# Who turns two of the ten blocks of a head's probabilities in the second layer

## The chip, the cores and the metric

One core of a Trainium2 chip runs the whole program. The metric is the time on the device in microseconds, the median of several runs; lower is better. A core has five engines with instruction queues of their own, which meet only at semaphores: TensorE (PE, the matrix unit; PEld are its weight loads), VectorE (DVE), ScalarE (ACT), GpSimd (POOL) and SyncE (SP, which here only starts DMAs). SBUF is the on-chip memory of 128 partitions, PSUM the memory of eight banks into which PE writes; DVE and ACT can read both.

## What is computed

A residual stack of two layers on 512 tokens of width 1024, with 8 heads of 128. Layer 0 is block-sparse attention, which with two blocks of 256 keys comes to causal attention, with rotary q and k. Layer 1, the second layer, is the forgetting attention. Cut to what matters:

```python
# layer 1, x is (1, 512, 1024)
hdn = rms_norm(x, norm_g[1])
proj = hdn @ b_w_in                          # q, k, v, z of 8 heads, and a forget logit for each head
q, k = rms_norm(q, b_q_norm), rms_norm(k, b_k_norm)
c = cumsum(log_sigmoid(f_logit + b_f_bias))  # along the tokens
s = q @ k.T * 128 ** -0.5 + (c[:, None] - c[None, :])   # causal: keys up to the query
y = softmax(s) @ v
x = x + (y * silu(z)) @ w_out[1]             # all in float32
```

## The kernel before

**Numbers.** The products are float32 in accuracy but are made of three products each of a high and a low part: for an operand X, ACT writes `X_hi`, the value rounded to PE's format, and DVE or POOL writes `X_lo`, the rest. `three` (L379 to L381) issues hi*hi, hi*lo, lo*hi.

**Tiles.** The 512 tokens are four tiles of 128. A head's scores are causal: query tile t has keys 0 to 128 (t + 1), so a head has ten blocks of 128x128. The probabilities lie in SBUF as `probs`, query tiles one after the other, queries on the partitions. For the product with v, keys must lie on the partitions, so each block is turned: `turn_probs` (L488) lets PE multiply it with an identity (L495), ten times, into the PSUM banks of `PT_AT`, grouped by key tile: group 0 is key tile 0 (512 columns), group 1 key tile 1 (384), group 2 key tiles 2 and 3 (256 + 128 columns next to each other in bank 5). Each group raises `p_turned`. ACT's `split_probs` copies a group from PSUM to `pT_hi` (L715, `pThi_set`), DVE's `split_probs` subtracts that from the group for `pT_lo` (L988, `pTlo_set`), and PE's `values` waits for all three groups and makes y in bank 3 (L509).

**The loop.** Each engine runs its own `period(layer, h, s)`: head 0 apart, then a hardware loop over heads 1 to 6 with two of them in a body, then `last` for head 7. In one period an engine works on the attention of head h, on the projection of head h + 1 and on the weights of head h + 2:
- PE: qkv of head h + 1 for token tiles 0 and 1, `scores` of head h, qkv for tiles 2 and 3, `turn_probs`, `zproj` (the gate z of head h + 1), `values`. qkv of a tile waits until `norm_qk` two tiles before it has freed its bank (`qkn_set`), and tile 0 of a head for its weights (`wlo_set`).
- DVE: `gate_y` of head h - 1, `split_qk` (L954, qkT_lo), `split_v` and `norm_qk` (L902, L919) of tile 0, `maxima` (L972), the same for tile 1, `invert_sums`, `low_y`, `silu_part` (L1013, L1017), `split_v` and `norm_qk` of tile 2, `split_v` of tile 3, `split_probs`, `norm_qk` of tile 3, and `turn_qk` (L947): q and k of head h + 1 turned from `qkn` into PSUM in sixteen STREAM_TRANSPOSE instructions. Each of them moves one block row and column of 32 partitions by 32 columns, for eight such squares at once.
- ACT: `split_qk` (L699, qkT_hi), `split_y` (L727, yT_hi), `read_qkv` of tile 0 (L684, sums of squares, and L693, v_hi) and of tile 1, `exps` (L706) and `normalise` (L722) which make the probabilities in the order of query tiles 3, 2, 1, 0 (`probs_set` each), `read_qkv` of tiles 2 and 3, `split_probs`, with the eight chunks of `split_w` (L638, w_hi of head h + 2) spread between; chunks 6 and 7 stand behind `split_probs`.
- POOL: the rstd of each tile (L1185, L1187, from ACT's sums to DVE's `norm_qk`), the eight chunks w_lo (L1160), and `mask_bias` (L1252), which adds the row of c to the causal mask for the maxima of the next head.

`r_row` is an SBUF buffer of 128x512, filled once and read in layer 0 alone (`scale_z`, L910).

Of the kernel before, what the change touches and what calls it, by code (L numbers as in the profile page):

```python
# [12 lines left out]
P = 128  # L13
SEQ = 512
DM = 1024
HEADS = 8
LAYERS = 2
TILES = SEQ // P
# [17 lines left out]
ALU = mybir.AluOpType  # L36
ACT = mybir.ActivationFunctionType
# [5 lines left out]
PT_AT = {0: (3, 0), 1: (4, 0), 2: (5, 0), 3: (5, 256)}  # L43
P_COL = {t: sum(P * (u + 1) for u in range(t)) for t in range(TILES)}
# [2 lines left out]
POOL_FIRST = {1: 2, 2: 1, 4: 2, 6: 2, 7: 1}  # L47
DVE_FIRST = (0, 3, 5)
NEXT_W = ((3, 4), (5, 6), (7,), ())
QUAD = 32  # L50
QUADS = P // QUAD


def build_trunk(nc, x, norm_g, w_out, a_w_in, a_q_norm, a_k_norm, b_w_in, b_f_bias, b_q_norm,
                b_k_norm, rope_cos, rope_sin, out):
    with ExitStack() as ctx:
# [3 lines left out]
        def sem(name):  # L60
            return ctx.enter_context(nc.semaphore(name))
# [22 lines left out]
        probs = sb("probs", [P, TRI])  # L84
        pT_hi = sb("pT_hi", [P, TRI], F32R)
# [79 lines left out]
        rinv_set = sem("rinv_set")  # L165
        probs_set = sem("probs_set")
        p_turned = sem("p_turned")
        pThi_set = sem("pThi_set")
        pTlo_set = sem("pTlo_set")
        y_done = sem("y_done")  # L170
# [24 lines left out]
        def f32(ap):  # L195

            return ap.bitcast(F32)
# [58 lines left out]
        def scaled_count(layer, t):  # L256

            return (TILES - UNSCALED + t if layer else t - UNSCALED) + 1

        def heads_loop(eng, layer, first, period, last):  # L260

# [112 lines left out]
        def _(pe):  # L374
# [113 lines left out]
            def turn_probs(layer, h):  # L488
                g = HEADS * layer + h
                pe.wait_ge(probs_set, TILES * (g + 1))  # L490
                for js in PT_GROUPS:
                    for j in js:
                        bank, col = PT_AT[j]
                        for t in range(j, TILES):
                            mm = pe.transpose(banks[:, bank, col + (t - j) * P:col + (t - j + 1) * P],  # L495
                                              probs[:, P_COL[t] + j * P:P_COL[t] + (j + 1) * P], ident[:, :])
                    mm.then_inc(p_turned, 1)
# [123 lines left out]
        def _(act):  # L621
# [87 lines left out]
            def split_probs(layer, h):  # L709
                g = HEADS * layer + h  # L710
                for n, js in enumerate(PT_GROUPS):
                    w = sum(SEQ - j * P for j in js)
                    c = PT_COL[js[0]]
                    act.wait_ge(p_turned, 3 * g + n + 1)
                    act.activation(pT_hi[:, c:c + w], banks[:, PT_AT[js[0]][0], 0:w], ACT.Copy).then_inc(pThi_set, 1)  # L715

            def normalise(layer, h):
                g = HEADS * layer + h
# [115 lines left out]
        def _(dve):  # L834
# [59 lines left out]
            def split_v(layer, h, s, t):  # L894
                a = TILES * (HEADS * layer + h) + t
                dve.wait_ge(vhi_set, a + 1)
                v = banks[:, qkv_bank(layer, h, t), 2 * P:3 * P]
                if unscaled(layer, t):
                    dve.scalar_tensor_tensor(out=v_lo[:, s, t, :], in0=v, scalar=r_raw[:, t:t + 1], in1=f32(v_hi[:, s, t, :]),
                                             op0=ALU.mult, op1=ALU.subtract).then_inc(vlo_set, 1)  # L900
                else:
                    dve.tensor_tensor(v_lo[:, s, t, :], v, f32(v_hi[:, s, t, :]), ALU.subtract).then_inc(vlo_set, 1)  # L902
# [9 lines left out]
            def norm_qk(layer, h, t):  # L912

                a = TILES * (HEADS * layer + h) + t
                dve.wait_ge(rstd_set, a + 1)
                wait(dve, qkn_set, a - 1)
                if layer == 1:
                    for m in range(2):
                        last = dve.scalar_tensor_tensor(out=qkn[:, t, m, :], in0=banks[:, qkv_bank(layer, h, t), m * P:(m + 1) * P],  # L919
                                                        scalar=rstd[:, t % 2, m:m + 1], in1=cos_t[:, 0, m, :],  # L920
                                                        op0=ALU.mult, op1=ALU.mult)
                    last.then_inc(qkn_set, 1)
                    return
                for m in range(2):
                    swapped = banks[:, qkv_bank(layer, h, t), m * P:(m + 1) * P].rearrange("p (a n) -> p a n", a=2)[:, ::-1, :]
                    dve.scalar_tensor_tensor(out=rot[:, t % 2, m].rearrange("p (a n) -> p a n", a=2), in0=swapped,
                                             scalar=rstd[:, t % 2, m:m + 1],
                                             in1=sin_t[:, t, m].rearrange("p (a n) -> p a n", a=2),
                                             op0=ALU.mult, op1=ALU.mult).then_inc(rot_set, 1)
                dve.wait_ge(rot_set, 4 * a + 2)  # L930
                for m in range(2):
                    part = banks[:, qkv_bank(layer, h, t), m * P:(m + 1) * P]
                    dve.scalar_tensor_tensor(out=part, in0=part, scalar=rstd[:, t % 2, m:m + 1], in1=cos_t[:, t, m],
                                             op0=ALU.mult, op1=ALU.mult).then_inc(rot_set, 1)
                dve.wait_ge(rot_set, 4 * a + 4)
                dve.tensor_tensor(qkn[:, t, :, :], banks[:, qkv_bank(layer, h, t), 0:2 * P].rearrange("p (m n) -> p m n", m=2),
                                  rot[:, t % 2, :, :], ALU.add).then_inc(qkn_set, 1)
# [44 lines left out]
            def split_probs(layer, h):  # L982
                g = HEADS * layer + h
                for n, js in enumerate(PT_GROUPS):
                    w = sum(SEQ - j * P for j in js)
                    c = PT_COL[js[0]]
                    dve.wait_ge(pThi_set, 3 * g + n + 1)
                    dve.tensor_tensor(pT_lo[:, c:c + w], banks[:, PT_AT[js[0]][0], 0:w], f32(pT_hi[:, c:c + w]),  # L988
                                      ALU.subtract).then_inc(pTlo_set, 1)

            def gate_y(layer, h):

# [108 lines left out]
            def period(layer, h, s):  # L1101
                begin(layer, h)
                split_v(layer, h + 1, 1 - s, 0)
                norm_qk(layer, h + 1, 0)
                maxima(layer, h)
                if layer == 0:
                    scale_z(layer, h)
                split_v(layer, h + 1, 1 - s, 1)
                norm_qk(layer, h + 1, 1)
                invert_sums(layer, h)  # L1110
                if layer == 1:
                    late_y(layer, h)
                for n in range(4):
                    silu_part(layer, h, n)
                split_v(layer, h + 1, 1 - s, 2)
                norm_qk(layer, h + 1, 2)
                split_v(layer, h + 1, 1 - s, 3)
                split_probs(layer, h)
                norm_qk(layer, h + 1, 3)
                turn_qk(layer, h + 1)  # L1120
# [198 lines left out]
```

## Time and profile before

| what | us |
|---|---|
| median of 3 runs | 547.85 |
| lowest and highest run | 547.60, 548.28 |
| the profiled execution, its own time | 548.04 |
| span of the profiled execution | 546.0 |
| PE busy / DVE busy in the span | 538.5 / 411.2 |
| ACT busy / POOL busy in the span | 293.3 / 301.6 |
| granted clock of PE, mean | 0.999 |

The time of a run lies about 2 us above the span, which begins with the first instruction of the program and ends with the last. Busy times are sums over the whole program; what counts is which engine waits for which at the place of the change, and for that the rows below go through one head in order of time. The second layer's loop takes from about 313 us to 502 us of the span. A row of the timeline is one instruction, or several of the same line in a row with their common length.

### The profile page before, as it was taken

What the parts mean: (1) busy time and instruction counts of PE and PEld (TensorE: products, weight loads), DVE (VectorE), ACT (ScalarE), POOL (GpSimd) and SP (SyncE); (2) the same over time, 40 slices, a digit from 0 to 9 for tenths busy, and PEclk for the clock granted to TensorE, in tenths of its full rate; (3) what the DMA queues carried; (4) which work ended last, traced back from release to release, by engine and by line L of the source; (5) the groups of instructions that cost most, each with busy time, mean ns of one, the idle gap of its engine ahead of it and who ended that gap; (6) DMA issues with size and microseconds to landing.
All of it is one profiled execution on the core that took longest, in us unless ns stands there. A gap on an engine that the chain in (4) does not pass through costs nothing.

```text
span 546.0 us, 9781 instructions
## 1 busy us (share of the span) xinstructions
PE 538.5 (99%) x2963; PEld 498.4 (91%) x2963; DVE 411.2 (75%) x1042; ACT 293.3 (54%) x863; POOL 301.6 (55%) x357
## 2 busy tenths in 40 slices
PE   6999999999999999999999999999999999999998
PEld 5999999999999999888898999999999999998887
DVE  4678999999999999973563777878787878788331
ACT  6748282928282828272545473737374747464400
POOL 3874564646464646453645486747474747476300
PEclk9999999999999999999999999999999999999999
DMA  9914323231313131223513345525241534232021
GB/s 262 250 27 127 101 59 97 59 97 58 96 58 96 58 96 59 95 86 118 128 27 80 97 102 74 120 61 130 52 121 54 116 57 121 73 105 84 26 96 59
DMA packets 78540, 50.22 MB, mean 92 GB/s; under 512 B 4256, under 2 KB 71592, under 8 KB 78512
## 3 DMA queue, kind: packets, MB, share of 16 engines
q1 hardware_dynamic: 78496, 49.87, 33.8%
q8 instruction: 14, 0.23, 0.2%
q14 instruction: 14, 0.11, 0.1%
q10 hardware_dynamic: 16, 0.00, 0.0%
HBM read 47.75 MB, written 2.12 MB: 91 GB/s over the span
## 4 chain that ended last, share of the span: by engine, by line
PE 97%; DMA 1%; ACT 0%; DVE 0%; SPq 0%; issue 0%
PE banks L379 27%; PE banks L381 27%; PE banks L380 27%; PE banks L509 6%; PE banks L495 3%; PE banks L484 2%; PE banks L483 2%; PE banks L482 2%; DMA first_raw<-in_a_w_in_dram 1%; PE banks L416 1%; PE banks L536 0%; PE banks L535 0%; ACT hT_hi L670 0%; PE banks L467 0%; SPq L333 0%; DVE w_lo L885 0%
## 5 line engine op out<-in xcount | busy, mean ns | idle before, releaser
L1160 POOL TENSOR_TENSOR w_lo<-w_raw,w_hi 128x512 fp32r<-128x512 f32 x146 | 188.4, 1305 | 84.0 <-ACT w_hi L638 84.0
L379 PE MATMUL banks<-w_hi,hT_hi 128*128 128x384 f32 x512 | 173.5, 339 | 0.5 <-DVE w_lo L885 0.3
L381 PE MATMUL banks<-w_hi,hT_lo 128*128 128x384 f32 x512 | 171.8, 336 | 0.0
L380 PE MATMUL banks<-w_lo,hT_hi 128*128 128x384 f32 x512 | 171.8, 335 | 0.0
L947 DVE STREAM_TRANSPOSE banks<-qkn 32x256 f32<-32x256 f32 x240 | 109.4, 456 | 3.6
L379 PEld LDWEIGHTS banks<-w_hi,hT_hi 128*128 128x128 f32 x512 | 96.7, 189 | 2.3 <-DVE w_lo L885 0.7
L380 PEld LDWEIGHTS banks<-w_lo,hT_hi 128*128 128x128 f32 x512 | 96.7, 189 | 0.6
L381 PEld LDWEIGHTS banks<-w_hi,hT_lo 128*128 128x128 f32 x512 | 96.5, 189 | 0.0
L684 ACT ACTIVATE junk<-banks 128x128 bf16<-128x128 f32 x128 | 34.0, 272 | 112.0 <-PE banks L381 111.8
L638 ACT ACTIVATE w_hi<-w_raw 128x512 fp32r<-128x512 f32 x148 | 89.0, 638 | 8.9 <-PE banks L381 5.4
L1013 DVE RECIPROCAL gz<-gz 128x128 f32<-128x128 f32 x64 | 54.3, 908 | 0.7 <-ACT gz L736 0.7
L379 PE MATMUL banks<-w_hi,yT_hi 128*128 128x512 f32 (+1 forms) x136 | 51.8, 381 | 0.0
L381 PE MATMUL banks<-w_hi,yT_lo 128*128 128x512 f32 (+1 forms) x136 | 51.3, 377 | 0.0
L380 PE MATMUL banks<-w_lo,yT_hi 128*128 128x512 f32 (+1 forms) x136 | 51.2, 377 | 0.0
L379 PE MATMUL banks<-hT_hi,w_hi 128*128 128x512 f32 x128 | 51.1, 399 | 0.0
L381 PE MATMUL banks<-hT_hi,w_lo 128*128 128x512 f32 x128 | 50.0, 390 | 0.0
L380 PE MATMUL banks<-hT_lo,w_hi 128*128 128x512 f32 x128 | 49.9, 390 | 0.0
L1187 POOL TENSOR_TENSOR rstd<-msq,power 128x2 f32<-128x2 f32 x64 | 45.2, 705 | 5.0
L706 ACT ACTIVATE probs<-probs,negmax 128x512 f32<-128x512 f32 (+1 forms) x64 | 35.2, 553 | 6.6 <-DVE negmax L972 5.7
L699 ACT ACTIVATE qkT_hi<-banks 128x512 fp32r<-128x512 f32 x32 | 17.5, 603 | 37.3 <-DVE banks L947 37.3
L1185 POOL TENSOR_TENSOR msq<-ssq,eps 128x2 f32<-128x2 f32 x32 | 6.4, 200 | 55.0 <-ACT junk L684 55.0
L1185 POOL TENSOR_TENSOR msq<-ssq,eps_raw 128x2 f32<-128x2 f32 x32 | 7.2, 224 | 53.5 <-ACT junk L684 53.5
(119 smaller groups left out, 915.9 us busy)
## 6 DMA issues: line engine op xcount, KB each, us to landing
w_raw<-in_b_w_in_dram SPq DMA_DIRECT2D x64, 256.0 KB, 3.6
w_raw<-in_a_w_in_dram SPq DMA_DIRECT2D x52, 256.0 KB, 2.9
w_raw<-in_w_out_dram SPq DMA_DIRECT2D x32, 256.0 KB, 2.7
first_raw<-in_a_w_in_dram SPq DMA_DIRECT2D x12, 256.0 KB, 5.7
cos_t<-c_rows SPq DMA_DIRECT2D x8, 256.0 KB, 3.6
out_dram<-xs SPq DMA_DIRECT2D x7, 256.0 KB, 2.0
xs<-in_x_dram SPq DMA_DIRECT2D x3, 512.0 KB, 5.9
xs<-in_x_dram SPq DMA_DIRECT2D x2, 256.0 KB, 3.1
```

The lines of the kernel that those rows point to most:

```text
L379: pe.matmul(dst, ah, bh, start=first and m == 0, stop=False)
L380: pe.matmul(dst, ah, bl, start=False, stop=False)
L381: mm = pe.matmul(dst, al, bh, start=False, stop=last and m == n - 1)
L509: mm = pe.matmul(banks[:, Y_BANK, j * P:SEQ], a[:, s, j, :], b[:, PT_COL[j]:PT_COL[j] + w], start=n == 0, stop=n == len(work) - 1)
L638: act.activation(w_hi[:, slot, k, :], raw, ACT.Copy).then_inc(whi_set, 1)
L684: sq = act.activation(junk[:, m, :], banks[:, qkv_bank(layer, h, t), m * P:(m + 1) * P], ACT.Square, scale=SCALE, accum_out=ssq[:, t % 2, ...
L699: act.activation(qkT_hi[:, m, :], banks[:, QT_BANK + m, :], ACT.Copy).then_inc(qkThi_set, 1)
L706: act.activation(part, part, ACT.Exp, bias=negmax[:, t:t + 1], scale=-1.0, accum_out=rowsum[:, t:t + 1]).then_inc(exp_set, 1)
L947: at = dve.transpose(turned[:, :, :, a * QUAD:(a + 1) * QUAD], tokens[:, :, :, b * QUAD:(b + 1) * QUAD])
L1013: dve.reciprocal(part, part).then_inc(ez1_set, 1)
L1160: pool.tensor_tensor(w_lo[:, slot, k, :], raw, f32(w_hi[:, slot, k, :]), ALU.subtract).then_inc(wlo_set, by)
L1187: pool.tensor_tensor(rstd[:, t % 2, :], msq[:, t % 2, :], power[:, :], ALU.pow).then_inc(rstd_set, 1)
```

## The change

In heads 0 to 6 of layer 1, the two blocks of query tile 3 with key tiles 2 and 3 are no longer turned by PE. DVE turns them: `turn_last_probs` is a new function with sixteen transposes of 32 partitions by two squares of 32 columns, from `probs` into columns 128 to 384 of `r_row`, which raises `last_turned`. It stands behind `norm_qk` of tile 2 and ahead of `split_v` of tile 3, and waits until query tile 3 of the probabilities is normalised. PE's `turn_probs` leaves out the two blocks. Group 2 is now 128 columns in PSUM and 256 columns in `r_row`, so ACT and DVE split it in two instructions; ACT's second one waits for `last_turned`. Group 2's signals `pThi_set` and `pTlo_set` are raised by the second one. Layer 0 and head 7 are as before. FIRST_BY_DVE = 2 is the first key tile that DVE turns.

```diff
--- before.py
+++ after.py
@@ -47,6 +47,7 @@
 POOL_FIRST = {1: 2, 2: 1, 4: 2, 6: 2, 7: 1}
 DVE_FIRST = (0, 3, 5)
 NEXT_W = ((3, 4), (5, 6), (7,), ())
+FIRST_BY_DVE = 2
 QUAD = 32
 QUADS = P // QUAD
 
@@ -165,6 +166,7 @@
         rinv_set = sem("rinv_set")
         probs_set = sem("probs_set")
         p_turned = sem("p_turned")
+        last_turned = sem("last_turned")
         pThi_set = sem("pThi_set")
         pTlo_set = sem("pTlo_set")
         y_done = sem("y_done")
@@ -257,6 +259,14 @@
 
             return (TILES - UNSCALED + t if layer else t - UNSCALED) + 1
 
+        def late_part(js):
+
+            return r_row[:, 0:P] if js[0] == 1 else r_row[:, P:3 * P]
+
+        def by_dve(layer, h):
+
+            return layer == 1 and not (isinstance(h, int) and h == HEADS - 1)
+
         def heads_loop(eng, layer, first, period, last):
 
 
@@ -492,6 +502,8 @@
                     for j in js:
                         bank, col = PT_AT[j]
                         for t in range(j, TILES):
+                            if by_dve(layer, h) and t == TILES - 1 and j >= FIRST_BY_DVE:
+                                continue
                             mm = pe.transpose(banks[:, bank, col + (t - j) * P:col + (t - j + 1) * P],
                                               probs[:, P_COL[t] + j * P:P_COL[t] + (j + 1) * P], ident[:, :])
                     mm.then_inc(p_turned, 1)
@@ -712,7 +724,12 @@
                     w = sum(SEQ - j * P for j in js)
                     c = PT_COL[js[0]]
                     act.wait_ge(p_turned, 3 * g + n + 1)
-                    act.activation(pT_hi[:, c:c + w], banks[:, PT_AT[js[0]][0], 0:w], ACT.Copy).then_inc(pThi_set, 1)
+                    late = P * sum(j >= FIRST_BY_DVE for j in js) if by_dve(layer, h) else 0
+                    hi = act.activation(pT_hi[:, c:c + w - late], banks[:, PT_AT[js[0]][0], 0:w - late], ACT.Copy)
+                    if late:
+                        act.wait_ge(last_turned, h + 1)
+                        hi = act.activation(pT_hi[:, c + w - late:c + w], late_part(js), ACT.Copy)
+                    hi.then_inc(pThi_set, 1)
 
             def normalise(layer, h):
                 g = HEADS * layer + h
@@ -985,8 +1002,30 @@
                     w = sum(SEQ - j * P for j in js)
                     c = PT_COL[js[0]]
                     dve.wait_ge(pThi_set, 3 * g + n + 1)
-                    dve.tensor_tensor(pT_lo[:, c:c + w], banks[:, PT_AT[js[0]][0], 0:w], f32(pT_hi[:, c:c + w]),
-                                      ALU.subtract).then_inc(pTlo_set, 1)
+                    late = P * sum(j >= FIRST_BY_DVE for j in js) if by_dve(layer, h) else 0
+                    lo = dve.tensor_tensor(pT_lo[:, c:c + w - late], banks[:, PT_AT[js[0]][0], 0:w - late],
+                                           f32(pT_hi[:, c:c + w - late]), ALU.subtract)
+                    if late:
+                        part = slice(c + w - late, c + w)
+                        lo = dve.tensor_tensor(pT_lo[:, part], late_part(js), f32(pT_hi[:, part]), ALU.subtract)
+                    lo.then_inc(pTlo_set, 1)
+
+            def turn_last_probs(layer, h):
+
+                g = HEADS * layer + h
+                dve.wait_ge(probs_set, TILES * g + 1)
+                row = P_COL[TILES - 1]
+                for js in ((1,), (2, 3)):
+                    if js[0] < FIRST_BY_DVE:
+                        continue
+                    n = len(js)
+                    tokens = probs[:, row + js[0] * P:row + (js[-1] + 1) * P].rearrange("p (j c) -> p j c", j=n)
+                    keys = late_part(js).rearrange("p (j c) -> p j c", j=n)
+                    for a in range(QUADS):
+                        for b in range(QUADS):
+                            turned = dve.transpose(keys[b * QUAD:(b + 1) * QUAD, :, a * QUAD:(a + 1) * QUAD],
+                                                   tokens[a * QUAD:(a + 1) * QUAD, :, b * QUAD:(b + 1) * QUAD])
+                turned.then_inc(last_turned, 1)
 
             def gate_y(layer, h):
 
@@ -1114,6 +1153,8 @@
                     silu_part(layer, h, n)
                 split_v(layer, h + 1, 1 - s, 2)
                 norm_qk(layer, h + 1, 2)
+                if by_dve(layer, h):
+                    turn_last_probs(layer, h)
                 split_v(layer, h + 1, 1 - s, 3)
                 split_probs(layer, h)
                 norm_qk(layer, h + 1, 3)
```

On DVE, head 0 of layer 1, from the reciprocals of the gate to the turning of q and k, before:

```order
L1013 RECIPROCAL gz<-gz 128x128 x4
L1017 TENSOR_TENSOR gz<-banks,gz 128x512
L902 TENSOR_TENSOR v_lo<-banks,v_hi 128x128
L919 SCALAR_TENSOR_TENSOR qkn<-banks,rstd,cos_t 128x128 x2
L902 TENSOR_TENSOR v_lo<-banks,v_hi 128x128
L988 TENSOR_TENSOR pT_lo<-banks,pT_hi 128x512
L988 TENSOR_TENSOR pT_lo<-banks,pT_hi 128x384 x2
L919 SCALAR_TENSOR_TENSOR qkn<-banks,rstd,cos_t 128x128 x2
L947 STREAM_TRANSPOSE banks<-qkn 32x8x32 x16
```

The same stretch now (line numbers of the changed kernel):

```order
L1052 RECIPROCAL gz<-gz 128x128 x4
L1056 TENSOR_TENSOR gz<-banks,gz 128x512
L919 TENSOR_TENSOR v_lo<-banks,v_hi 128x128
L936 SCALAR_TENSOR_TENSOR qkn<-banks,rstd,cos_t 128x128 x2
L1026 STREAM_TRANSPOSE r_row<-probs 32x2x32 x16
L919 TENSOR_TENSOR v_lo<-banks,v_hi 128x128
L1006 TENSOR_TENSOR pT_lo<-banks,pT_hi 128x512
L1006 TENSOR_TENSOR pT_lo<-banks,pT_hi 128x384
L1006 TENSOR_TENSOR pT_lo<-banks,pT_hi 128x128
L1010 TENSOR_TENSOR pT_lo<-r_row,pT_hi 128x256
L936 SCALAR_TENSOR_TENSOR qkn<-banks,rstd,cos_t 128x128 x2
L964 STREAM_TRANSPOSE banks<-qkn 32x8x32 x16
```

Sixteen transposes from `probs` stand ahead of v_lo of tile 3 and of all pT_lo, and the third pT_lo is two instructions. The loop over heads 1 to 6 has the same order.

On ACT, head 0 of layer 1, the probabilities' high parts and what follows, before:

```order
L693 ACTIVATE v_hi<-banks 128x128
L715 ACTIVATE pT_hi<-banks 128x512
L715 ACTIVATE pT_hi<-banks 128x384 x2
L638 ACTIVATE w_hi<-w_raw 128x512 x2
L734 ACTIVATE gz<-banks 128x512
```

And now:

```order
L705 ACTIVATE v_hi<-banks 128x128
L728 ACTIVATE pT_hi<-banks 128x512
L728 ACTIVATE pT_hi<-banks 128x384
L728 ACTIVATE pT_hi<-banks 128x128
L731 ACTIVATE pT_hi<-r_row 128x256
L650 ACTIVATE w_hi<-w_raw 128x512 x2
L751 ACTIVATE gz<-banks 128x512
```

The 256-wide copy from `r_row`, which waits for DVE, stands ahead of the last two chunks of the weights. On PE the ten turns in a row are eight, at the same place.

## Rows read from the trace of the kernel before

**Rows 1.** The page: busy time by engine; the chain that ended last.

```profile
PE 538.5 (99%) x2963; PEld 498.4 (91%) x2963; DVE 411.2 (75%) x1042; ACT 293.3 (54%) x863; POOL 301.6 (55%) x357
...
PE 97%; DMA 1%; ACT 0%; DVE 0%; SPq 0%; issue 0%
```

**Rows 2.** Stretch 310 to 500: length, busy PE, PEld, DVE, ACT, POOL; clock; DMA.

```profile
310.00:500.00 190.00, 190.00 (x1076) 180.35 (x1075) 148.81 (x389) 110.12 (x341) 123.44 (x145) 1.00 0.37 87
```

**Rows 3.** Timeline of PE: start, length, instruction, shapes, count.

```profile
377.66 1.25 PE L495 MATMUL banks<-ident,probs 128*128 128x128 f32 x10
378.67 0.48 PE L379 MATMUL banks<-hT_hi,w_hi 128*128 128x512 f32 x1
...
384.20 0.56 PE L509 MATMUL banks<-pT_hi,v_hi 128*128 128x512 f32 x2
...
386.12 0.34 PE L379 MATMUL banks<-w_hi,hT_hi 128*128 128x384 f32 x1
...
394.47 0.39 PE L482 MATMUL banks<-qkT_hi 128*128 128x512 f32 x1
...
492.42 0.56 PE L509 MATMUL banks<-pT_hi,v_hi 128*128 128x512 f32 x2
...
501.82 0.39 PE L482 MATMUL banks<-qkT_hi 128*128 128x512 f32 x1
```

**Rows 4.** Timeline of DVE in head 2; in brackets idle time before, and releaser.

```profile
376.54 0.61 DVE L919 SCALAR_TENSOR_TENSOR qkn<-banks,rstd,cos_t 128x128 f32<-128x128 f32 x2
378.68 0.29 DVE L902 TENSOR_TENSOR v_lo<-banks,v_hi 128x128 fp32r<-128x128 f32 x1 [1.54 <-ACT v_hi L693]
379.17 1.62 DVE L988 TENSOR_TENSOR pT_lo<-banks,pT_hi 128x512 fp32r<-128x512 f32 x3 [0.20 <-ACT pT_hi L715]
380.71 0.60 DVE L919 SCALAR_TENSOR_TENSOR qkn<-banks,rstd,cos_t 128x128 f32<-128x128 f32 x2
381.34 7.50 DVE L947 STREAM_TRANSPOSE banks<-qkn 32x256 f32<-32x256 f32 x16
...
389.51 1.29 DVE L954 TENSOR_TENSOR qkT_lo<-banks,qkT_hi 128x512 fp32r<-128x512 f32 x2
...
392.52 0.61 DVE L919 SCALAR_TENSOR_TENSOR qkn<-banks,rstd,cos_t 128x128 f32<-128x128 f32 x2 [0.76 <-POOL rstd L1187]
395.38 0.69 DVE L972 CUSTOM_DVE_ANT_0 probs<-banks,sin_t 128x512 f32<-128x512 f32 x1 [2.24 <-issue]
```

**Rows 5.** Groups by shape, 310 to 500: count, busy us, mean ns, idle before.

```profile
L947 DVE STREAM_TRANSPOSE banks<-qkn 32x256 f32<-32x256 f32 x113 | 51.5, 456 | 1.7
L988 DVE TENSOR_TENSOR pT_lo<-banks,pT_hi 128x384 fp32r<-128x384 f32 x14 | 7.1, 547 | 0.0
L988 DVE TENSOR_TENSOR pT_lo<-banks,pT_hi 128x512 fp32r<-128x512 f32 x7 | 4.8, 692 | 1.4 <-ACT pT_hi L715 1.4
...
L972 DVE CUSTOM_DVE_ANT_0 probs<-banks,sin_t 128x512 f32<-128x512 f32 x7 | 4.8, 687 | 12.2 <-issue 12.2
...
L972 DVE CUSTOM_DVE_ANT_0 probs<-banks,sin_t 128x128 f32<-128x128 f32 x7 | 2.0, 285 | 0.0
...
L722 ACT ACTIVATE probs<-probs,rinv 128x256 f32<-128x256 f32 x7 | 3.5, 495 | 0.0
```

**Rows 6.** Timeline of ACT in head 2.

```profile
371.77 1.91 ACT L722 ACTIVATE probs<-probs,rinv 128x512 f32<-128x512 f32 x4
...
389.85 0.63 ACT L727 ACTIVATE yT_hi<-gz 128x512 f32 x1
390.64 0.28 ACT L684 ACTIVATE junk<-banks 128x128 bf16<-128x128 f32 x1 [0.16 <-PE banks L381]
```

**Rows 7.** Timeline of POOL in head 2: w_lo 6 and 7.

```profile
380.50 2.55 POOL L1160 TENSOR_TENSOR w_lo<-w_raw,w_hi 128x512 fp32r<-128x512 f32 x2 [0.58 <-ACT w_hi L638]
```

**Rows 8.** Timeline of PE and DVE in head 0.

```profile
313.31 0.39 PE L482 MATMUL banks<-qkT_hi 128*128 128x512 f32 x1
...
316.38 0.06 DVE L971 MEMSET gate<- 1x1 f32 x1 [2.92 <-POOL sin_t L1252]
...
324.64 0.61 DVE L919 SCALAR_TENSOR_TENSOR qkn<-banks,rstd,cos_t 128x128 f32<-128x128 f32 x2 [0.78 <-POOL rstd L1187]
...
330.10 0.56 PE L509 MATMUL banks<-pT_hi,v_hi 128*128 128x512 f32 x2
```

## The prediction

> **What bounds the kernel now.** I read the page first. TensorE (PE) is busy for 99% of the span and makes 97% of the chain that ended last [rows 1]. In the second layer it never waits: between 310 and 500 us it is busy for all 190.00 us [rows 2]. So work taken from PE shortens the run one for one, as long as nothing makes PE wait instead. VectorE (DVE) is busy for 75% of the span and for 148.81 us of those 190, so it is idle for 22% of them [rows 1, 2]. The reader should look next at where that idle time lies, because only idle time at the right place can pay for new work.
>
> I call the heads of the second layer head 0 to head 7. One round of the loop takes PE 27.05 us: the values of head 2 start at 384.20, those of head 6 at 492.42, and (492.42 - 384.20) / 4 = 27.05 [rows 3]. The rows of DVE in head 2 show three large pieces of idle time in such a round: 1.54 us before v_lo of query tile 3, 0.76 us before norm_qk 0, 2.24 us before the maxima [rows 4]. The second one is a wait for POOL, which itself starts behind ACT and DVE: it moves along with a delay and absorbs nothing.
>
> **PE's part.** Ten turns of probabilities take from 377.66 to 378.67, 0.10 us each [rows 3]; the first product behind them also ends later than usual (0.48 us), so I count 0.105. Two of ten go in heads 0 to 6: 0.21 us a head, **1.5 us** in all. Nothing hides this gain, since PE is the bound. PE's round becomes 26.84 us. Head 7 stays as it is.
>
> **DVE's part.** Sixteen transposes of 32x64 a head are new. The trace has only the 32x256 kind: 456 ns each, and sixteen of them last 7.50 us, so (7.50 - 0.46) / 15 = 0.470 us from start to start: they don't overlap at all [rows 4, 5]. Other instructions of DVE do: three pT_lo of 692, 547 and 547 ns take 1.54 us up to the next start, 0.08 us less for each than their length [rows 4, 5]. What does a narrow transpose cost? The maxima take 285 ns for 128 columns and 687 for 512, which is 1.05 ns a column and 151 ns fixed [rows 5]. Taking 192 columns off a wide transpose gives 0.470 - 0.201 = 0.27 us. If its fixed part were those 151 ns too, a column would cost 1.19 ns and a narrow one 0.24 us. If narrow ones overlapped as pT_lo does, it would be 0.151 + 0.067 - 0.08 = 0.14 us, the lower end. At the upper end a narrow one costs as much as a wide one, 0.47 us; with nothing that makes columns free here I leave that end only a trace of a chance. I take 0.26 us, between 0.24 and 0.27 and nearer to the straight subtraction, thus **4.2 us a head**.
>
> That transposes don't overlap is also what the Trainium skill says in "VectorE: DVE Perf Modes", section "Two Vector instructions with no wait between them": an instruction whose output starts in another group of 32 partitions than the one before is held until everything before it has finished. By that rule, the trace's 470 ns agree, and the new loop, which also changes that group at each step, would be held too. The same page's section on the TRN2 errata has 58 cycles plus the columns for work from SBUF to SBUF; as an estimate from it a narrow one would be 127 ns and the whole 2.0 us a head, and the run would gain the full 1.5 us. The 456 ns of the wide ones speak against it.
>
> The third pT_lo and the third pT_hi (128x384) become a 128-wide and a 256-wide instruction each. From start to start that is 0.20 + 0.34 us on DVE where one 384-wide takes 0.47: 0.07 us more. On ACT the 256-wide copy from SBUF has 495 ns by the row of the same shape [rows 5], in place of two thirds of the old 384-wide one: some 0.2 us more. The wait for probabilities ahead of the transposes costs nothing: they are ready at 371.77 + 1.91 = 373.68 [rows 6], DVE comes at 377.07.
>
> **A steady head, walked through (times of head 2).** The transposes start behind norm_qk 2, at 377.07, and end at 381.25. v_lo, pT_lo 0, pT_lo 1 and the two parts follow in steps of 0.20, 0.61, 0.47 and 0.20 us, so the last part starts at 382.73 and pT_lo is complete at 383.15. norm_qk 3 starts 0.34 us after that part, at 383.07 instead of 380.71: 2.37 us late. PE wants pT_lo at 384.20 - 0.21 = 383.99 [rows 3, 4]. Covered, with 0.8 us to spare. Behind it turn_qk (7.50 us) moves from 381.34 to 383.71, and qkT_lo ends at 393.17 instead of 390.80; PE's scores want it at 394.47 - 0.21 = 394.26. Covered. ACT's yT_hi goes to 392.22 and its read of tile 0 to 392.75, 2.11 late (before it had waited some 0.26 us for PE) [rows 6]; so norm_qk 0 goes from 392.52 to 394.63, and DVE is ready for the maxima at 395.15. PE's scores allow them at 395.38 - 0.21 = 395.17. **DVE's round, through ACT and POOL, is then 26.83 us, PE's 26.84.** All the absorbing idle time is used up, and a head that starts late can't catch up any more.
>
> The third pT_hi waits for DVE until 381.25. Queued behind it on ACT stand w_hi 6 and 7, and behind those on POOL w_lo 6 and 7 (380.50 to 383.05) [rows 7]. They move by 1.9 us to about 385.0; PE needs them for the next tile at 386.12 - 0.21 = 385.91 [rows 3]. Covered with 0.9 us in a head on time, but with only 0.1 us in one where PE has already waited for pT_lo.
>
> **Head 0 is not steady.** There PE's scores start at 313.31 but DVE's maxima at 316.4, because they wait 2.92 us for the bias that POOL makes: 3.1 us behind, where it is 0.9 us later on. norm_qk 2 starts at 324.64, PE's values at 330.10 [rows 8]. With the change the transposes run from 325.17 to 329.37, pT_lo is complete 1.90 us later, at 331.27, and PE starts its values at 331.32 instead of 330.10 - 0.21 = 329.89. **PE waits 1.4 us**, once. From then on PE sits right behind pT_lo, and since DVE's round equals PE's it stays there, without further waits in heads 1 to 6 if 0.26 is right.
>
> **Head 7** has less work for PE between values and scores: from 492.42 to 501.82 are 9.40 us, in the loop from 384.20 to 394.47 10.27 [rows 3]. From a complete pT_lo to a complete qkT_lo DVE takes 393.17 - 383.15 = 10.02 us. Behind a head 6 at the edge these scores wait up to 0.6 us. I take 0.5, since six heads have won back some hundredths each.
>
> **Sum:** -1.5 + 1.4 + 0.5 = +0.4 us on the profiled run of 548.04 (span 546.0), which lies 0.19 us over the median of the runs, 547.85. On the median that is **548.3 us**. A measurement of this kernel can tell some 0.2%, 1.1 us; this is less.
>
> How it hangs on the narrow transpose: each 0.01 us of it is 0.16 us in head 0, and above 0.26 it is another 0.16 us in each of the six heads behind.
> - 0.14 us: no waits, -1.5.
> - 0.24 us: 1.1 us in head 0; DVE wins back 0.3 us a head, so no wait in head 7: -0.4.
> - 0.27 us: 1.6 + 6 x 0.15 + 0.6 - 1.5 = +1.6.
> - 0.28 us: 1.75 + 6 x 0.31 + 0.6 - 1.5 = +2.7.
>
> **Rivals.**
> 1. The loop through DVE becomes the bound (slower). Its place is the wait for pTlo_set ahead of the values, in each of heads 1 to 6. It decides from about 0.265 us a transpose, or from any 0.1 us a round that my walk lacks. For it: the straight subtraction gives 0.27 and my margin is 0.01 us. Against it: the fixed part of every other kind is 151 ns, which gives 0.24. It gives 549.0 to 550.6, in the middle 549.6. Chance 0.32.
> 2. Narrow transposes are cheap and overlap, 0.14 to 0.20 us. PE waits 0.4 us at most, in head 0: 546.4 to 546.8. For it: other instructions of DVE overlap. Against it: no wide transpose does. Chance 0.10. The Trainium skill, "Vector Engine (DVE) Microarchitecture Reference", section 5.2, has about 1.04 ns a column and 75 ns for each instruction, an estimate of 142 ns with the same outcome; no row here shows it for transposes.
> 3. POOL's w_lo 7 is late rather than pT_lo. Its place is PE's first tile behind the values. It needs 0.1 us more on ACT or POOL than I have and gives 0.1 to 0.3 us a head: 548.6 to 550. Chance 0.05, half of it beyond 1.1 us.
> 4. That the change does not do what it says is excluded by the order of the instructions: eight turns on PE and sixteen transposes on DVE stand where ten turns stood.
>
> **How the numbers follow.** Forecast (547.2 to 548.9) 0.53, rival 1 0.32, rival 2 0.10, rival 3 0.05. Faster by over 0.2% (below 546.75) is nearly all of rival 2: 0.09. Slower by over 0.2% (above 548.95) is rival 1 nearly whole and half of rival 3: 0.33. Within 0.2%: 0.58. The range takes the forecast, rival 1 up to a transpose of 0.28 us less a little, and the slower half of rival 2: 546.7 to 550.4.
>
> **What would show it.** Right: transposes from probs 245 to 255 ns long and 0.26 us apart behind norm_qk 2; PE's first wait ahead of the values of head 0, 1.4 us, released by DVE's pT_lo; none or tiny ones in heads 1 to 6; one ahead of the scores of head 7; DVE's idle time before the maxima near 0 where it was 2.24 us; DVE's busy share up from 75% to about 80%. Wrong: no wait in head 0 (rival 2), waits ahead of the values of every head (rival 1), or waits ahead of the first tile with POOL as releaser (rival 3).

## The result, and the profile after

The changed kernel takes 551.86 us (median of 6 runs, 551.56 to 552.67) beside 547.92 for the kernel before (6 runs, 547.60 to 549.10). The ratio is 1.007, with a 95% interval of 1.0057 to 1.0083: it is 3.9 us slower. I had forecast 548.3 and at most 550.4.

The page of the changed kernel shows PE at 98% and DVE at 80%. The chain that ended last was PE for 97% before [rows 1]; now DVE and POOL hold a share of it:

```profile
PE 538.7 (98%) x2949; PEld 495.4 (90%) x2949; DVE 440.8 (80%) x1161; ACT 293.2 (53%) x870; POOL 302.3 (55%) x357
...
PE 58%; DVE 20%; POOL 9%; issue 8%; ACT 3%; DMA 1%; POOLq 0%; SPq 0%; ACTq 0%; DVEq 0%
```

The waits of PE's weight loads say where. Each row gives what was waited for, then the us in total, how often, and the longest. Seven waits for the last part of pT_lo stand ahead of the values, one for qkT_lo ahead of the scores:

```profile
PEld banks L521 <- DVE pT_lo L1010: 5.9, 7, 2.1
...
PEld banks L492 <- DVE qkT_lo L971: 0.8, 1, 0.8
```

PE's timeline shows when the values of a head start: here for heads 0, 1, 2 and 6, and in the last row the scores of head 7. The idle time in brackets is how PE arrives there, after a weight load that had stood waiting.

```profile
331.80 0.68 PE L521 MATMUL banks<-pT_hi,v_hi 128*128 128x512 f32 x2 [1.72 <-DVE pT_lo L1010]
...
359.12 0.68 PE L521 MATMUL banks<-pT_hi,v_hi 128*128 128x512 f32 x2 [0.15 <-DVE pT_lo L1010]
...
386.43 0.68 PE L521 MATMUL banks<-pT_hi,v_hi 128*128 128x512 f32 x2 [0.17 <-DVE pT_lo L1010]
...
495.74 0.50 PE L521 MATMUL banks<-pT_hi,v_hi 128*128 128x512 f32 x1 [0.22 <-DVE pT_lo L1010]
...
505.75 0.50 PE L492 MATMUL banks<-qkT_hi 128*128 128x512 f32 x1 [0.34 <-DVE qkT_lo L971]
```

Head 0 starts its values at 331.80, where the prediction's walk had 329.89 without a wait: 1.9 us. From 331.80 to 495.74 are six rounds of 27.32 us, where PE alone would need the 26.84 of the prediction: 0.48 us in each, 2.9 together. Head 7's scores come 10.01 us after head 6's values, before it was 9.40 [rows 3]: 0.6. With 1.4 us taken from PE (measured below) that is 1.9 + 2.9 + 0.6 - 1.4 = +4.0, and the runs say 3.9.

What is slow in the round of DVE? Its groups by shape between 310 and 505 us (count, busy us, mean ns, idle before):

```profile
L1026 DVE STREAM_TRANSPOSE r_row<-probs 32x64 f32<-32x64 f32 x112 | 26.4, 236 | 1.4
...
L1010 DVE TENSOR_TENSOR pT_lo<-r_row,pT_hi 128x256 fp32r<-128x256 f32 x7 | 7.9, 1122 | 0.0
```

The transposes are a little cheaper than forecast, 236 ns long where the prediction had 245 to 255. The subtraction of 256 columns, which I had put at 0.34 us from start to start, takes 1122 ns. The timeline of head 2 shows what runs beside it: DVE in the first fence, POOL in the second, ACT in the third.

```profile
379.78 3.97 DVE L1026 STREAM_TRANSPOSE r_row<-probs 32x64 f32<-32x64 f32 x16
383.78 0.29 DVE L919 TENSOR_TENSOR v_lo<-banks,v_hi 128x128 fp32r<-128x128 f32 x1
383.99 1.34 DVE L1006 TENSOR_TENSOR pT_lo<-banks,pT_hi 128x512 fp32r<-128x512 f32 x3
385.24 1.13 DVE L1010 TENSOR_TENSOR pT_lo<-r_row,pT_hi 128x256 fp32r<-128x256 f32 x1
386.30 0.60 DVE L936 SCALAR_TENSOR_TENSOR qkn<-banks,rstd,cos_t 128x128 f32<-128x128 f32 x2
```

```profile
380.62 1.30 POOL L1201 TENSOR_TENSOR w_lo<-w_raw,w_hi 128x512 fp32r<-128x512 f32 x1 [0.16 <-ACT w_hi L650]
...
384.80 2.72 POOL L1201 TENSOR_TENSOR w_lo<-w_raw,w_hi 128x512 fp32r<-128x512 f32 x2 [1.95 <-ACT w_hi L650]
...
386.04 1.48 POOL L1201 TENSOR_TENSOR w_lo<-w_raw,w_hi 128x512 fp32r<-128x512 f32 x1
```

```profile
383.78 0.42 ACT L731 ACTIVATE pT_hi<-r_row 128x256 fp32r<-128x256 f32 x1 [1.52 <-DVE r_row L1026]
384.10 0.61 ACT L650 ACTIVATE w_hi<-w_raw 128x512 fp32r<-128x512 f32 x1
```

The second POOL row is w_lo 6 and w_lo 7 together, the third is w_lo 7 alone. w_lo 6 runs from 384.80 to 386.09. DVE's subtraction starts inside it, at 385.24, and ends at 386.37, 0.28 us behind it. w_lo 7, which starts before DVE is done, takes 1.48 us, and the two chunks together last 2.72 us where they lasted 2.55 [rows 7]. In all seven heads the subtraction starts about 0.45 us behind w_lo 6 and takes 1.10 to 1.13 us. The change itself brings the two together: ACT now waits for DVE's transposes before its last pT_hi, and w_hi 6 and 7 are queued behind that, so POOL gets w_hi 6 just before DVE reaches the subtraction.

### The profile page after: what moved, and what is told of

Same layout as the page of the kernel before. It is cut to its first block, busy times and chain, and to the rows that moved or that the text cites. A ratio compares the mean times of both kernels' runs of the same rounds, so it can differ in the third digit from the quotient of the medians.

```text
span 550.1 us, 9885 instructions
## 1 busy us (share of the span) xinstructions
PE 538.7 (98%) x2949; PEld 495.4 (90%) x2949; DVE 440.8 (80%) x1161; ACT 293.2 (53%) x870; POOL 302.3 (55%) x357
## 4 chain that ended last, share of the span: by engine, by line
PE 58%; DVE 20%; POOL 9%; issue 8%; ACT 3%; DMA 1%; POOLq 0%; SPq 0%; ACTq 0%; DVEq 0%
PE banks L389 16%; PE banks L391 16%; PE banks L390 16%; DVE banks L964 10%; POOL w_lo L1201 6%; DVE r_row L1026 4%; PE banks L521 3%; PE banks L507 2%; POOL rstd L1228 2%; DVE qkn L936 2%; DVE pT_lo L1010 1%; DVE pT_lo L1006 1%; DMA first_raw<-in_a_w_in_dram 1%; PE banks L494 1%; PE banks L493 1%
```

## The experiments

**Theory A**: the 256-wide subtraction, with both inputs in SBUF, stands still while POOL's w_lo runs. **Rival B**: `r_row` is slow to read, by its place in SBUF or because it was just written. **Rival C**: pT_hi, which ACT has just written, is slow to read, so the loss has nothing to do with where the first input lies.

Besides the runs' time I give the **stretch** from the start of head 0's scores to that of head 7's, read from PE's timeline. It leaves out the start of the program, which varies between executions: head 0's scores start between 312.76 us (experiment 6) and 314.52 us (experiment 3) in the profiled ones. The mean granted clock of PE is 1.00 in every profiled execution. The stretch of the kernel before is 501.82 - 313.31 = 188.51 us [rows 3, 8], that of the changed kernel 505.75 - 313.33 = 192.42.

Each ratio is to the kernel before on the same chip. Its medians there were 547.89 us for experiments 1 to 4, 548.21 for 5 to 8, 548.04 for 9 and 10, and 548.74 for 11. Experiments 2, 3 and 4 were run once, so their times carry no interval.

**1. PSUM in the place of r_row.** One line:

```diff
-            return r_row[:, 0:P] if js[0] == 1 else r_row[:, P:3 * P]
+            return banks[:, QT_BANK, 2 * P:3 * P] if js[0] == 1 else banks[:, QT_BANK, 0:2 * P]
```

> The changed kernel with one line other: DVE turns the two blocks into PSUM bank 6 (free between the splitting of q and k and their next turning) and no longer into r_row in SBUF, so the 256-wide pT_lo has one input in PSUM and one in SBUF. In the changed kernel this instruction takes 1122 ns where its columns explain 420; in all seven heads it starts 0.45 us after a w_lo of POOL, which also reads two SBUF inputs, and ends 0.28 us after it. Theory A (a DVE instruction with two SBUF inputs waits for a running one of POOL): 420 ns here, DVE's round 27.32 - 0.70 = 26.62 us, below PE's 26.84; PE waits 1.2 us ahead of the values of head 0 and not in heads 1 to 6; in all -1.5 + 1.2 + 0 to 0.2, so 547.6 us. Rival B (r_row is slow to read, by its place or because it was just written): the same, 547.6. Rival C (pT_hi, just written by ACT, is what is slow to read): 1.1 us for the instruction as before, 551.9 us.

Measured: 550.37 us (549.68 to 551.31), ratio 1.004 (1.0027 to 1.0053), stretch 190.54. The groups of DVE:

```profile
L1010 DVE TENSOR_TENSOR pT_lo<-banks,pT_hi 128x256 fp32r<-128x256 f32 x7 | 2.9, 414 | 0.0
...
L1026 DVE STREAM_TRANSPOSE banks<-probs 32x64 f32<-32x64 f32 x112 | 28.7, 256 | 1.6
```

The subtraction falls from 1122 to 414 ns with POOL beside it as before (in head 2 it starts at 386.10, inside a w_lo that starts at 385.62 and takes 1.29 us). It still reads pT_hi, so C is out. A and B both fit. But the time is far from the 547.6 that I expected. The transposes into PSUM take 256 ns instead of 236, 0.33 us more for sixteen, and the first of them starts 0.64 us behind norm_qk 2 instead of 0.53. These 0.44 us bring DVE's round from the expected 26.62 to some 27.05 us, still 0.21 over PE's. 1.65 in head 0 + 6 x 0.21 + 0.6 in head 7 - 1.4 = +2.1, and the stretch has grown by 2.0. Half of the loss is gone, and what is left is a new cost that the experiment itself brought in.

**2. POOL's chunks 6 and 7 cut to 16 columns** in the second layer (the rest of these w_lo isn't computed):

```diff
+                    if layer == 1 and k >= 6 and not (isinstance(h, int) and h < 2):
+                        pool.tensor_tensor(w_lo[:, slot, k, 0:16], raw[:, 0:16], f32(w_hi[:, slot, k, 0:16]),
+                                           ALU.subtract).then_inc(wlo_set, by)
+                        continue
```

> The changed kernel with POOL's last two chunks of w_lo of layer 1 (from head 2's weights on) cut to 16 of 512 columns; the other columns keep old values, so this part of the computation is left out. DVE's instructions are those of the changed kernel. Theory A: with POOL idle at that time the 256-wide pT_lo from r_row takes 420 ns, PE has no waits ahead of the values of heads 1 to 6, 547.6 us. Rivals B and C: it stays at 1.1 us, 551.9 us.

Measured: 547.92 us in one run, stretch 188.42. DVE's row in head 2, and POOL's two short chunks:

```profile
383.77 0.42 DVE L1010 TENSOR_TENSOR pT_lo<-r_row,pT_hi 128x256 fp32r<-128x256 f32 x1
```

```profile
383.33 0.22 POOL L1202 TENSOR_TENSOR w_lo<-w_raw,w_hi 128x16 fp32r<-128x16 f32 x1 [1.78 <-ACT w_hi L650]
383.99 0.28 POOL L1202 TENSOR_TENSOR w_lo<-w_raw,w_hi 128x16 fp32r<-128x16 f32 x1 [0.43 <-ACT w_hi L650]
```

DVE's program is unchanged to the last instruction, `r_row` and `pT_hi` lie where they lay, and the subtraction takes 416 ns in the mean of seven (414 to 417). So B and C are out, and A is what is left. PE waits for pT_lo once, in head 0, for 1.0 us on PE's timeline. This run costs 4.0 us of stretch less than the changed kernel: that is the price of the standing still, in the seven heads together. It is less than 7 x 0.70 us because without it PE's own round is the longer one again. What is left without it is 188.42 against 188.51, -0.1 us, where the prediction's sum said +0.4.

**3. One input instead of two** (the subtraction is left out; pT_lo becomes a rounded copy):

```diff
-                        lo = dve.tensor_tensor(pT_lo[:, part], late_part(js), f32(pT_hi[:, part]), ALU.subtract)
+                        lo = dve.tensor_scalar(pT_lo[:, part], late_part(js), 1.0, None, ALU.mult)
```

> The changed kernel with the 256-wide pT_lo made from r_row alone (times 1.0, the subtraction of pT_hi is left out), so it reads one SBUF input. Theory A (two SBUF inputs are needed for the wait): 300 to 420 ns, 547.5 us. Rival B (r_row is slow): 1.1 us, 551.9. Rival C (pT_hi is slow): like A.

Measured: 552.43 us in one run, stretch 191.61. In head 2, DVE and then POOL:

```profile
386.25 1.00 DVE L1010 TENSOR_SCALAR pT_lo<-r_row 128x256 fp32r<-128x256 f32 x1
```

```profile
385.80 2.60 POOL L1201 TENSOR_TENSOR w_lo<-w_raw,w_hi 128x512 fp32r<-128x512 f32 x2 [1.89 <-ACT w_hi L650]
```

I had expected the loss to vanish with the second input. It didn't: 992 ns in the mean of seven, ending 0.15 us behind POOL's first chunk. B would give this as well, but experiment 2 has ruled B out. So this instruction with one input stands still too, and "two inputs in SBUF" was too narrow. What it costs beside an idle POOL no run shows. Yet the transposes, which also go from SBUF to SBUF, don't stand still: sixteen of them took 3.97 us in the changed kernel with POOL's chunk at 380.62 in the middle of them, and all 112 of the run take 222 to 242 ns. The reciprocals of the gate, which read one input in SBUF and write to SBUF, are not held up either. Of the changed kernel in head 2, the last of four on DVE and then the chunk of POOL inside which it starts and ends:

```profile
377.35 0.89 DVE L1052 RECIPROCAL gz<-gz 128x128 f32<-128x128 f32 x1
```

```profile
377.00 1.29 POOL L1201 TENSOR_TENSOR w_lo<-w_raw,w_hi 128x512 fp32r<-128x512 f32 x1 [0.90 <-ACT w_hi L650]
```

The Trainium skill has the rule, in "SBUF — State Buffer", section "SBUF: two separate sides": DVE and GpSimd share one pair of ports, the one that starts first keeps it for its whole instruction and the other is fully blocked. On DVE's side the rule applies to instructions with two SBUF inputs, beside an instruction of GpSimd that reads SBUF, and to those in a two-port performance mode, which the page says a float32 copy from SBUF to SBUF triggers. The trace agrees for two inputs (1122 ns, and 416 with POOL idle). The 992 ns of this run fit the second kind, but no run shows which mode the instruction runs in.

**4. Another buffer** (`rot`) in the place of `r_row`:

```diff
-            return r_row[:, 0:P] if js[0] == 1 else r_row[:, P:3 * P]
+            flat = rot[:, :, :, :].rearrange("p a b n -> p (a b n)")
+            return flat[:, 0:P] if js[0] == 1 else flat[:, P:3 * P]
```

> The changed kernel with another SBUF buffer, rot (128x512, not in use any more at that time), in place of r_row. Theory A: nothing changes, 1.12 us for the 256-wide pT_lo, 551.9 us. Rival B as the place of r_row: 420 ns and 547.6 us. Rival C: 1.1 us, 551.9 us.

Measured: 551.69 us in one run, stretch 192.45. The subtraction's mean is the same to the nanosecond, so it is not the place of `r_row`:

```profile
L1011 DVE TENSOR_TENSOR pT_lo<-rot,pT_hi 128x256 fp32r<-128x256 f32 x7 | 7.9, 1122 | 0.0
```

**5. Head 0 turned by PE**, heads 1 to 6 as changed:

```diff
-            return layer == 1 and not (isinstance(h, int) and h == HEADS - 1)
+            return layer == 1 and not isinstance(h, int)
...
-                        act.wait_ge(last_turned, h + 1)
+                        act.wait_ge(last_turned, h)
```

> The changed kernel, but head 0 keeps its ten turns on PE; heads 1 to 6 as changed. I read all from the stretch between the start of head 0's scores and that of head 7's, which the length of the start does not touch: 188.51 us before, 192.42 with the change. Theory: two separate costs, a wait of 1.9 us in head 0 (DVE is late there already) and DVE's round of 27.32 us against PE's 26.84. Then without head 0: no wait in head 0 and head 1, 0.2 in head 2, 0.48 us in each of heads 3 to 6, 0.6 ahead of head 7's scores, less six savings of 0.21: +1.5 us, stretch 190.0, 549.4 us. Rival (the wait in head 0 is only the first place where DVE's longer round shows, and comes back later in full): stretch 192, 551.5 us.

Measured: 549.98 us (548.90 to 550.77), ratio 1.0025 (1.0015 to 1.0036), stretch 190.01. The 1.9 us of head 0 are gone and don't come back later, as the rival had it. The waits that remain are those of a DVE round longer than PE's:

```profile
PEld banks L521 <- DVE pT_lo L1010: 3.1, 5, 0.7
```

**6. Both, 1 and 5 together:** PSUM, and head 0 by PE.

> e1_psum without head 0. DVE's round was 27.06 us there, PE's is 26.84. Theory: the lag grows 0.22 us a head, a margin of 0.63 us holds it until head 4, then 0.03 + 0.22 + 0.22 in heads 4 to 6 and 0.6 ahead of head 7's scores, less 1.26: stretch 188.3, 547.7 us, no change that can be measured. Rival (an independent cost is left in the new transposes, such as a slower PE): stretch 190, 549.4 us.

Measured: 547.83 us (547.48 to 549.12), ratio 0.9994 (0.9985 to 1.0003), stretch 188.42. PE's gain of 1.2 us is cancelled by its waits behind DVE's round of 27.05 us, 0.2 longer than PE's own, and by the 0.6 us ahead of head 7's scores.

**7. PE's part alone:** in the kernel before, two turns are left out in heads 0 to 6 and nothing is done in their place (two blocks of the probabilities are not turned).

```diff
                         for t in range(j, TILES):
+                            if layer == 1 and t == TILES - 1 and j >= 2 and not (isinstance(h, int) and h == HEADS - 1):
+                                continue
```

> The kernel before with PE's two turns left out in heads 0 to 6 of layer 1 and nothing in their place, so two of ten blocks of the probabilities are stale. It measures what PE's part alone is worth. All theories: 14 x 0.105 us, stretch 187.0, 546.4 us. A rival for my sum (PE's part is worth less because something else holds PE's round at 27.05): stretch 188.5.

Measured: 546.20 us (546.12 to 546.83), ratio 0.996 (0.9946 to 0.9974), stretch 187.13. That is 1.38 us of stretch for 14 turns, 0.099 us each.

**8. Both, 2 and 5 together:** POOL's chunks short (again the rest of these w_lo isn't computed), head 0 by PE.

> e2_pool_short without head 0: both costs taken away, DVE's new transposes and instructions all there. POOL's last two chunks of w_lo are cut to 16 columns, left out of the computation. Theory: no waits of PE in heads 0 to 7, six savings of 0.21: stretch 187.25, 546.6 us. Rival (the sixteen transposes cost PE time in themselves): stretch above 188.

Measured: 546.72 us (546.54 to 547.61), ratio 0.9972 (0.9962 to 0.9982), stretch 187.32, and no wait of PE in the loop of the second layer. With head 0, which starts late, left to PE and nothing in DVE's way the idea does pay, in a kernel that is not complete: 12 turns x 0.099 = 1.2 us.

**9. A complete kernel that keeps POOL apart.** Heads 1 to 6 by DVE. ACT makes w_hi 6 and 7 ahead of its pT_hi, so POOL's w_lo 6 and 7 are over before the subtraction; `mask_bias` waits until it is done.

```diff
                 read_qkv(layer, h + 1, 1 - s, 3)
+                if by_dve(layer, h):
+                    split_w(layer, h + 2, s, (6, 7))
                 split_probs(layer, h)
-                split_w(layer, h + 2, s, (6, 7))
+                if not by_dve(layer, h):
+                    split_w(layer, h + 2, s, (6, 7))
...
                 pool.wait_ge(c_in, 16 * (h + 1))
+                if not isinstance(h, int) or h > 0:
+                    pool.wait_ge(pTlo_set, 3 * (HEADS + h))
```

> A whole kernel, nothing left out: heads 1 to 6 as changed, head 0 on PE; ACT makes w_hi 6 and 7 ahead of pT_hi, so POOL's w_lo 6 and 7 are over before DVE comes to the part of pT_lo from r_row, and POOL's next bias waits until pT_lo is complete. Theory: the 256-wide pT_lo takes 416 ns, DVE's round 27.32 - 0.70 = 26.62 us is below PE's 26.84, no waits in heads 1 to 6: six savings of 0.21, stretch from head 0's to head 7's scores 187.3 us (188.51 before), 546.7 us, 0.2% faster than before. Rival (the moved work of ACT and POOL comes late instead, by w_raw that isn't loaded yet or by the bias): waits of 0.3 us a head or more, stretch over 188.5.

Measured: 547.81 us (547.09 to 548.78), ratio 0.9996 (0.9988 to 1.0005), stretch 188.44 instead of 187.3. The subtraction takes 416 ns in every head, so that part is right. One head spoils it, head 2. Its rows on ACT:

```profile
379.44 0.63 ACT L650 ACTIVATE w_hi<-w_raw 128x512 fp32r<-128x512 f32 x1 [1.24 <-DMA w_raw<-in_b_w_in_dram]
381.65 0.63 ACT L650 ACTIVATE w_hi<-w_raw 128x512 fp32r<-128x512 f32 x1 [1.59 <-DMA w_raw<-in_b_w_in_dram]
382.19 1.13 ACT L728 ACTIVATE pT_hi<-banks 128x512 fp32r<-128x512 f32 x3
```

And on DVE:

```profile
382.81 1.35 DVE L1009 TENSOR_TENSOR pT_lo<-banks,pT_hi 128x512 fp32r<-128x512 f32 x3 [1.93 <-ACT pT_hi L728]
```

Chunks 6 and 7 of the weights are not there yet, ACT waits for their DMAs with pT_hi queued behind, and DVE and PE wait for pT_hi. That is the rival mechanism that the expectation names. It struck in one head of six, and cost 1.1 us of stretch, nearly the whole gain.

**10. The same with head 0 by DVE too.**

> The same with head 0 changed too. Theory: 1.5 us saved, 1.2 us of waiting in head 0, 0 to 0.2 us ahead of head 7's scores: stretch 188.2 to 188.4 us, 547.7 us. Rival as for e9.

Measured: 549.55 us (549.21 to 551.03), ratio 1.0036 (1.002 to 1.0051), stretch 190.32, 2 us more than expected. PE waits ahead of the values twice, in head 0, as expected, and in head 2, where ACT again waits for the weights' DMAs (1.91 us for chunk 7):

```profile
PEld banks L521 <- DVE pT_lo L1013: 3.5, 2, 2.1
```

**11. POOL takes the subtraction itself.** Heads 1 to 6 by DVE's transposes. ACT makes w_hi 6, then pT_hi, then w_hi 7; POOL does w_lo 6, the 256 columns of pT_lo, then w_lo 7; PE waits for POOL's part as well. From the edit to the changed kernel, cut:

```diff
-                    if late:
-                        part = slice(c + w - late, c + w)
-                        lo = dve.tensor_tensor(pT_lo[:, part], late_part(js), f32(pT_hi[:, part]), ALU.subtract)
...
+                pool.wait_ge(pThi_set, 3 * (HEADS * layer + h) + 3)
+                pool.tensor_tensor(pT_lo[:, part], late_part(js), f32(pT_hi[:, part]),
+                                   ALU.subtract).then_inc(late_lo, 1)
```

> The complete computation, and a version meant to keep the gain. Heads 1 to 6 are turned as the change does, head 0 by PE as in the kernel before. The 256 columns of pT_lo that come from r_row are no longer DVE's: POOL subtracts them, between w_lo 6 and w_lo 7 (0.65 us by half of its 128x512 of 1.29). ACT makes w_hi 6 ahead of its pT_hi and w_hi 7 behind them, so that POOL's w_lo 6 is out of the way. PE waits for POOL's part too. If what was lost is DVE's subtraction standing still beside POOL (theory A), it is gone with the instruction, DVE's round falls to 26.4 us and PE's 26.85 binds in all of heads 1 to 6, head 2 too: stretch from head 0's scores to head 7's 187.3 us (kernel before 188.5), 546.7 us. Rival: POOL's w_lo 7 is late instead. It ends 0.7 us later than in the kernel before or more; PE needs it 1.7 us behind the start of the values, and with more than the 0.9 us of cover used up each head waits 0.1 to 0.5 us: stretch 188 to 190, 547.5 to 549.5 us. Second rival: w_raw is late in head 2 as in the run before, stretch 188.4, 547.8 us.

Measured: 547.40 us (546.74 to 547.93) beside 548.74 for the kernel before on the same chip, ratio 0.9978 (0.9969 to 0.9987), stretch 187.34 against 187.3 expected. The first row is the stretch from 310 to 500 us, with PE busy for all of it again as in [rows 2]; the others are POOL in head 3:

```profile
310.00:500.00 190.00, 190.00 (x1070) 180.16 (x1069) 167.84 (x484) 109.50 (x344) 126.86 (x150) 1.00 0.37 87
```

```profile
407.27 1.30 POOL L1203 TENSOR_TENSOR w_lo<-w_raw,w_hi 128x512 fp32r<-128x512 f32 x1
408.96 0.74 POOL L1296 TENSOR_TENSOR pT_lo<-r_row,pT_hi 128x256 fp32r<-128x256 f32 x1 [0.39 <-ACT pT_hi L734]
409.66 1.29 POOL L1203 TENSOR_TENSOR w_lo<-w_raw,w_hi 128x512 fp32r<-128x512 f32 x1
```

POOL's w_lo 7 ends at 410.95, and PE starts the values at 411.42 and needs it 1.7 us behind that, so there are 2.2 us to spare. Neither rival came true: PE has no wait in the loop, though ACT waits 0.83 us for chunk 6 in head 2. This version is 0.2% faster than the kernel before, little but clear of the noise. The 546.7 us expected were counted from a kernel before of 547.9, which here takes 548.74. Set against the changed kernel, which was not run beside it, its stretch is 5.1 us shorter.

## Why the prediction was wrong

- **PE's part, -1.5 us: right, slightly high.** Experiment 7 measures 1.38 us of stretch, 0.099 us a turn where I had counted 0.105.
- **The transposes, 0.26 us apart: right, slightly dear.** 3.97 us for sixteen are 0.25 us apart, and they don't overlap, as the wide ones didn't. It gives back 0.16 us a head. ACT's copy of the 256 columns from `r_row`, put at 495 ns, takes 0.42 us.
- **Head 0's wait, 1.4 us: the mechanism right.** Measured 1.9, which is 1.4 - 0.16 + 0.70. Without the 0.70, in experiment 2, head 0's values start 1.2 us later than with no wait. Experiment 5, without the change in head 0, has that part gone.
- **Head 7's scores, 0.5 us: right**, 0.6 measured, and for the reason given.
- **The step that failed** is "From start to start that is 0.20 + 0.34 us on DVE where one 384-wide takes 0.47: 0.07 us more." I scaled it with the columns, by rows whose first input lies in PSUM [rows 5]. The new one has both inputs in SBUF, and it meets POOL's w_lo. It takes 1122 ns instead of the 416 that it takes beside an idle POOL (experiment 2): 0.70 us more in each head. The prediction moved w_lo 6 and 7 by 1.9 us to end at about 385.0 and asked only whether they would be ready in time, not what DVE would be doing beside them. Its own figures put w_lo 6 at 380.50 + 1.9 = 382.4 and the last part of pT_lo at 382.73, one inside the other.
- **Rival 1 therefore came true**, chance 0.32, and by its second condition, "any 0.1 us a round that my walk lacks": the walk lacked 0.70, less 0.16 won back by the transposes. DVE's round went from the forecast 26.83 to 27.32 us; 26.83 - 0.16 + 0.70 would be 27.37. Six rounds of 0.48 us are the 2.9 us that put the result beyond the range, whose upper end I had tied to the price of the transpose alone.
- **Rivals 2 and 3 didn't happen.** No transpose overlaps another (0.25 us apart, not 0.14 to 0.20), and no first tile behind the values waits for w_lo in the loop.

The trace of the kernel before could have told it. At the start of the program DVE and POOL both split weights from SBUF, DVE in the first fence and POOL in the second:

```profile
8.93 0.69 DVE L885 TENSOR_TENSOR w_lo<-first_raw,w_hi 128x512 fp32r<-128x512 f32 x1
...
12.56 3.05 DVE L885 TENSOR_TENSOR w_lo<-first_raw,w_hi 128x512 fp32r<-128x512 f32 x2
```

```profile
12.08 2.98 POOL L1160 TENSOR_TENSOR w_lo<-first_raw,w_hi 128x512 fp32r<-128x512 f32 x2 [0.16 <-ACT w_hi L638]
```

The same instruction of DVE takes 0.69 us while POOL is idle, and two take 3.05 us beside two of POOL's, which take 2.98 us themselves where two elsewhere take 2.56. That is a row of the new subtraction's own kind, both inputs in SBUF and POOL at work beside it, and I had priced it by others.

The loop itself has a sign of it too, in the other direction. In head 2 of the kernel before, a chunk of POOL starts while DVE's subtraction for yT_lo runs, which has both inputs in SBUF, and takes 1.43 us instead of 1.29:

```profile
371.53 0.69 DVE L1003 TENSOR_TENSOR yT_lo<-gz,yT_hi 128x512 f32 x1
```

```profile
371.94 1.43 POOL L1160 TENSOR_TENSOR w_lo<-w_raw,w_hi 128x512 fp32r<-128x512 f32 x1 [1.41 <-ACT w_hi L638]
```

## What to carry to other kernels

When an edit changes where an operand lies, price the instruction by a row with the same places of its inputs, not by one of the same width; look for the longest duration of such a row too, and at what ran beside it. When an edit moves a wait, ask of every instruction queued behind it not only whether it is still in time but what it will now run beside. And where two loops of engines are within hundredths of a microsecond of each other, let the range cover more than the one price you doubt: each tenth of a microsecond that the walk lacks counts once for each round.

## What the runs showed of the hardware

- A 128x256 subtraction of DVE with both inputs in SBUF that starts while POOL's subtraction of two SBUF tensors runs ends only after that: 1122 ns, where 416 ns is the price with POOL idle. With the first input in PSUM it takes 414 ns beside a running POOL.
- A multiplication of DVE by a constant, from one SBUF input to SBUF (128x256), also ends only after POOL's: 992 ns. Its price with POOL idle was not measured.
- POOL's next chunk, which starts while DVE's two-input subtraction still runs, takes 1.48 us instead of 1.29.
- Transposes of 32x64 from SBUF to SBUF (222 to 242 ns) and reciprocals of 128x128 from SBUF to SBUF (0.89 us inside a chunk of POOL) are not held up by POOL.
- The transposes take 236 ns into SBUF and 256 ns into PSUM, and start 0.25 and 0.27 us apart.
- Why the transposes and the reciprocals go free where the multiplication doesn't, no run here tells apart.
